# A modulation vector's last step taken from TensorE, and the vectors after it formed one place later

## The chip, the cores and the metric

The kernel runs as one program on one core of a Trainium2 chip. The metric is the device time of one execution in microseconds (us), median of three runs. Engines work side by side and meet only at semaphores: TensorE (PE in the rows; PEld is its weight load), VectorE (DVE), ScalarE (ACT), GpSimd (POOL) and SyncE (SP), whose only work here is to start transfers.

## The reference

Two blocks over 512 tokens of width 1024. The first is an attention and convolution block with a gate:

```python
x = first_block(x, p, ...)          # attention || conv, w_out, RMS norm, then x + sigmoid(x @ w_ple_gate) * e
c_act = jax.nn.silu(c)
for i in range(2):
    mod = c_act @ w_ada[i] + b_ada[i]                     # 6 vectors of 1024
    sh1, sc1, g1, sh2, sc2, g2 = jnp.split(mod, 6, axis=-1)
    h = modulate(rmsnorm(x, norm_mix_g[i]), sh1, sc1)     # h * (1 + sc1) + sh1
    m = fourier_mixer(h, w_fourier_out[0]) if i == 0 else retention_mixer(h, ...)
    x = x + g1[:, None, :] * m
    h = modulate(rmsnorm(x, norm_ffn_g[i]), sh2, sc2)
    x = x + g2[:, None, :] * swiglu(h, w_ffn_in[i], w_ffn_out[i])   # hidden width 2816
shf, scf = jnp.split(c_act @ w_ada_final + b_ada_final, 2, axis=-1)
return modulate(rmsnorm(x, final_norm_g), shf, scf)
```

There are so 14 modulation vectors of 1024 numbers, `mod[0]` to `mod[13]`: six for each layer and two for the end. Each is a 1024-vector times a 1024 x 1024 matrix of float32 (4 MB). `mod[4]` is `sc2` of layer 0, the scale of its second norm; `mod[5]` is `g2` of layer 0; `mod[11]` is `g2` of layer 1.

## The kernel before

**The weights' stream.** All weights of the matmuls lie in HBM in the order of their use, as 257 chunks of 128 x 1024 (512 KB, eight 128 x 128 weight tiles). A chunk c goes through four hands, in rings of four slots: SP loads it (`w_raw`, L346), ACT rounds it to a high part (`w_hi`, L455), POOL subtracts to get the low part in four quarters (`w_lo`, L423), and PE multiplies with both: three matmuls for each tile (lo x hi, hi x lo, hi x hi; L1785, L1788, L1789 for 512 columns, L1801 to L1805 for half tiles). SP starts the load of chunk c when POOL has finished chunk c-4; ACT splits chunk c when PE has begun chunk c-3; PE begins chunk c when all four quarters of its low part are there. Each engine runs its instructions in the written order, so SP is one queue: what stands behind a waiting load waits too.

**The modulation's stream.** The vectors' matrices come as 112 pieces of 512 KB (8 for a vector) through `ada_raw`, a ring of only two slots. A piece a is loaded by SP (L352) when VectorE has consumed piece a-2 (`ada_sum`). VectorE's step on a piece (`ada`: L992 for a vector's first, L995 for the others) multiplies the 128 x 1024 piece with one column of `cact` and adds it to `ada_acc`. After eight steps `ada_acc` holds 128 partial sums for each of the 1024 outputs, which must be summed over the partitions and turned into columns. Three ways stand in the kernel: vectors 0 to 3 (in the attention's loop) are transposed by PE (`ada_turn`); vector 4 goes through eight matmuls of 128 x 128 by one column (`ada_columns`, L1964), which stand between the tiles of the `ple` product, and VectorE adds the bias (`ada_out`, L1008); vectors 5 to 13 are turned in blocks by VectorE (`ada_fold`, L1030 transpose and L1031 sum), moved between partitions by sixteen small copies on ScalarE (`ada_move`, L796) and summed by VectorE (`ada_collect`, L1024 and L1025). The last way writes to a part of `cols`, the `ident` columns, that nobody reads after the attention.

**Where the pieces are loaded.** SP's program is written out: a load of a weight chunk, then as many pieces as stand with that chunk. `load(at, k)` does so for one chunk; `turns(n, chunks, k)` is a loop of n rounds; `until(c)` loads chunks alone. Vector 5's pieces (40 to 47) stand in the Fourier mixer, 48 to 95 with 48 chunks from `up0a`+10 on, 96 to 111 with 16 chunks from `up1a`+10 on.

**The stages.** attention (32 chunks), `out` (8), `ple` (2), `gate` (8), Fourier mixer `dft1`, `dft2`, `fout` (1, 4, 8), layer 0's swiglu `up0a` (24), `down0a` (12), `up0b` (20), `down0b` (10), retention (64), layer 1's swiglu (66). Counted from `up0a` as 0, `down0a` begins at chunk 24, `up0b` at 36, `down0b` at 56 and the retention at 66. In `down0b` (K = 10 tiles of hidden values by 8 output tiles) the first four output tiles run side by side and end at a quarter, a half, three quarters and the end of chunk 60 (from chunk 56: 32 products, then two for each tile); VectorE adds each to the residual (L1163), ScalarE squares it (L690), VectorE adds the squares (L1061). Here ScalarE's order is: the splits of chunks 60 to 64, then the first four squares, then the splits of 65 and on.

**VectorE's steps around the change.** In the mixer: two steps after `dft1`, one behind each of three Fourier groups, three before `fout`'s tiles, 8 in all (vector 5). In `up0a`: 24 steps; in `down0a`: 8 behind tiles 3 to 6; in `up0b`: 16 (4 for each of the first four rounds); in `down0b`: none. In `up1a`: 16.

Of the kernel before, what the change touches and what calls it, by code (L numbers as in the profile page):

```python
# [16 lines left out]
P = 128  # L17
# [88 lines left out]
for _name, _n in (("pre", 1), ("body", 7 * NH), ("post", 1), ("ada4", 1), ("ple", 1), ("four", 1), ("fshift", 1), ("edge", 1),  # L106
                  ("ffn0", 1), ("rnorm", 1),
                  ("ret", NH), ("ffn1", 1), ("final", 1)):
    AUX[_name] = _c
    _c += _n  # L110
# [28 lines left out]
def build(nc, W, ADA, XT, PT, COLS, DIST, ROPE, DECAY, OUT):  # L139
# [3 lines left out]
    with ctx:  # L143
# [197 lines left out]
        def _(sp):  # L341
# [103 lines left out]
        def _(act):  # L445
# [26 lines left out]
            def vector(g):  # L472

                return lambda m: mod[:, KD * g + m:KD * g + m + 1]

# [308 lines left out]
            for n in range(8):  # L784
                if n < 6:
                    split_w(flat, c0 + n + 4)
# [3 lines left out]

            def ada_move(g, at=flat):

                act.wait_ge(ada_folded, at("vector", g - 4))
                for b in range(4):
                    for q in range(4):
                        ins = act.activation(ada_quads[32 * q:32 * q + 32, :, b], ada_part[32 * b:32 * b + 32, q:32:4],  # L796
                                             ACT.Copy)
                ins.then_inc(ada_moved, 1)
# [17 lines left out]
            def swiglu(layer, v, t0):  # L816
                split_norm(4 + 2 * layer, 1 + 2 * layer, AUX[f"ffn{layer}"], t0, vector(6 * layer + 3),
                           CH[f"up{layer}a"])
                for part, n_hid in zip("ab", HALF):
# [5 lines left out]
                    if layer == 0:  # L825
                        n_pairs, g = (n_hid // 2 - first) // 2, 5 if first else 9
# [17 lines left out]
                    for n in range(n_hid):  # L844
                        if layer == 0 and part == "a" and n == 2:
                            ada_move(8)
# [125 lines left out]
        def _(dve):  # L972
# [43 lines left out]
            def ada_collect(g, at=flat):  # L1016

                dve.wait_ge(ada_moved, at("vector", g - 4))
# [367 lines left out]
            for m in range(KD):  # L1386
# [6 lines left out]
                if m == 2:  # L1393
                    ada_out(AUX["ada4"], 4)
# [67 lines left out]
            ada(k=2)  # L1462
# [10 lines left out]
            for g in range(NH):  # L1473
# [58 lines left out]
            def swiglu(layer, v, a_in, with_ada, t_in, g_in):  # L1532
                g0 = 6 * layer
                split_norm(f"ffn{layer}", v - 1, a_in, vector(g0 + 3), t_in, g_in, gain(2 + 2 * layer))
                for part, n_hid in zip("ab", HALF):
# [3 lines left out]
                    g = 5 + (0 if first else 4)  # L1539
                    if first:  # L1540
                        up_body(flat, t, j)
                    if with_ada:
                        n_pairs = (n_hid // 2 - first) // 2
                        began = steps[0]
                        with dve.Fori(0, n_pairs) as i:
                            at = At(i, tile=8, bank=2, hid=4, ada=8, adaslot=64, vector=1, eight=8, link=2)
                            ada_fold(g, at)
# [898 lines left out]
```

## Time and profile before

| | us |
|---|---|
| median of 3 runs (lowest, highest) | 1541.06 (1540.83, 1541.74) |
| the profiled execution's own time | 1540.15 |
| its span, first to last instruction | 1538.2 |
| PE busy | 1526.9 (99%) |
| POOL busy | 876.3 (57%) |
| DVE busy | 786.8 (51%) |
| ACT busy | 632.4 (41%) |

The profiled execution's span is 1.95 us shorter than its own time, and that time is 0.91 us below the median. TensorE's granted clock is 0.999 of full speed over the span. PE is busy nearly throughout, so a change counts only where PE's stream grows, shrinks or waits. PE's busy time counts the matmuls' full length, which overlap: a matmul of 512 columns is listed with 0.39 us, while the next one starts 0.23 us later. Gaps in PE's work are read best from starts.

### The profile page before, as it was taken

Reading aid. Unit: us, or ns where it says so; the run is one execution under the profiler, and the core shown is the slowest. Engines: PE = TensorE matmul, PEld = TensorE weight load, DVE = VectorE, ACT = ScalarE, POOL = GpSimd, SP = SyncE. Lnnn points to the kernel's source line nnn. Section 1 sums busy time; section 2 is a strip of 40 time slices with the busy share of each in tenths; the row PEclk is TensorE's granted clock in tenths of the full one; section 3 lists DMA queues with packets and bytes.
Section 4 is the critical chain, followed back from the end, with each engine's and each line's share of the span. In section 5 each row is a group of like instructions: output and inputs, shape, how many; then the busy total and the mean of one; then the engine's idle time right before and its main releaser. Section 6 shows DMA issues by size and latency. Waiting matters only on the chain.

```text
span 1538.2 us, 21352 instructions
## 1 busy us (share of the span) xinstructions
PE 1526.9 (99%) x7242; PEld 1276.9 (83%) x7242; DVE 786.8 (51%) x1176; ACT 632.4 (41%) x1038; POOL 876.3 (57%) x1040
## 2 busy tenths in 40 slices
PE   9999999999999999999999999999999999999997
PEld 7888888898888888888888888888889888888886
DVE  7887787876654544541554435356257454011113
ACT  7444444674533333323444334253345333122223
POOL 6555557556577766775454535526435766555551
PEclk9999999999999999999999999999999999999999
DMA  7544455335355555542232322213312553222321
GB/s 247 178 145 165 167 192 191 110 110 178 122 180 205 196 190 181 199 150 96 101 103 69 108 69 94 95 52 96 95 55 83 205 205 123 96 96 95 95 82 55
DMA packets 58267, 202.99 MB, mean 132 GB/s; under 512 B 6496, under 2 KB 8544, under 8 KB 58208
## 3 DMA queue, kind: packets, MB, share of 16 engines
q1 hardware_dynamic: 56912, 198.87, 37.8%
q10 hardware_dynamic: 1296, 3.30, 0.6%
q8 instruction: 40, 0.66, 0.2%
q14 instruction: 19, 0.16, 0.0%
HBM read 200.05 MB, written 2.10 MB: 131 GB/s over the span
## 4 chain that ended last, share of the span: by engine, by line
PE 78%; POOL 11%; issue 9%; ACT 0%; DMA 0%; DVE 0%; SPq 0%; POOLq 0%; DVEq 0%; ACTq 0%
PE banks L1785 21%; PE banks L1789 21%; PE banks L1788 21%; POOL w_lo L423 11%; PE banks L2270 2%; PE banks L2269 2%; PE banks L2266 2%; PE banks L1801 2%; PE banks L1804 2%; PE banks L1805 2%; PE banks L2306 1%; PE banks L2304 1%; PE banks L2305 1%; PE banks L2293 0%; PE banks L2292 0%
## 5 line engine op out<-in xcount | busy, mean ns | idle before, releaser
L423 POOL TENSOR_TENSOR w_lo<-w_raw,w_hi 128x256 fp32r<-128x256 f32 x1028 | 868.9, 877 | 627.8 <-ACT w_hi L455 627.7
L455 ACT ACTIVATE w_hi<-w_raw 128x1024 fp32r<-128x1024 f32 x257 | 269.9, 1057 | 582.6 <-PE banks L1785 518.8
L1785 PE MATMUL banks<-a_hi,w_lo 128*128 128x512 f32 x1224 | 479.2, 391 | 0.1
L1789 PE MATMUL banks<-a_hi,w_hi 128*128 128x512 f32 x1224 | 476.7, 389 | 0.0
L1788 PE MATMUL banks<-a_lo,w_hi 128*128 128x512 f32 x1224 | 476.6, 389 | 0.0
L1785 PEld LDWEIGHTS banks<-a_hi,w_lo 128*128 128x128 f32 x1224 | 230.1, 188 | 47.6 <-issue 0.8
L1789 PEld LDWEIGHTS banks<-a_hi,w_hi 128*128 128x128 f32 x1224 | 229.8, 188 | 47.8
L1788 PEld LDWEIGHTS banks<-a_lo,w_hi 128*128 128x128 f32 x1224 | 229.9, 188 | 47.3 <-issue 0.2
L1785 PE MATMUL banks<-b_hi,w_lo 128*128 128x512 f32 x562 | 219.6, 391 | 0.0
L1789 PE MATMUL banks<-b_hi,w_hi 128*128 128x512 f32 x562 | 218.8, 389 | 0.0
L1788 PE MATMUL banks<-b_lo,w_hi 128*128 128x512 f32 x562 | 218.8, 389 | 0.0
L995 DVE SCALAR_TENSOR_TENSOR ada_acc<-ada_raw,small,ada_acc 128x1024 f32<-128x1024 f32 x98 | 149.1, 1522 | 44.6 <-DMA ada_raw<-in_ADA 42.5
L1785 PEld LDWEIGHTS banks<-b_hi,w_lo 128*128 128x128 f32 x562 | 105.5, 188 | 22.9 <-DVE scr L1492 0.5
L1788 PEld LDWEIGHTS banks<-b_lo,w_hi 128*128 128x128 f32 x562 | 105.5, 188 | 21.9 <-issue 0.2
L1789 PEld LDWEIGHTS banks<-b_hi,w_hi 128*128 128x128 f32 x562 | 105.5, 188 | 21.9
L1163 DVE SCALAR_TENSOR_TENSOR X<-banks,mod,X 128x512 f32<-128x512 f32 x63 | 46.1, 748 | 146.8 <-PE banks L1789 146.7
L1520 DVE TENSOR_TENSOR scr<-scr,banks 128x512 f32<-128x512 f32 x44 | 30.2, 687 | 109.5 <-PE banks L1789 109.2
L1516 DVE SCALAR_TENSOR_TENSOR scr<-scr,banks 128x512 f32<-128x512 f32 x44 | 30.2, 687 | 102.2 <-ACT scr L807 102.2
L1528 DVE SCALAR_TENSOR_TENSOR b_lo<-scr,b_hi 128x512 f32 (+1 forms) x44 | 33.3, 757 | 52.1 <-ACT b_hi L814 52.1
L2269 PE MATMUL banks<-w_hi,a_lo 128*128 128x512 f32 x128 | 49.8, 389 | 0.0
L2266 PE MATMUL banks<-w_lo,a_hi 128*128 128x512 f32 x128 | 49.8, 389 | 0.0
L2270 PE MATMUL banks<-w_hi,a_hi 128*128 128x512 f32 x128 | 49.8, 389 | 0.0
(300 smaller groups left out, 1708.4 us busy)
## 6 DMA issues: line engine op xcount, KB each, us to landing
w_raw<-in_W SPq DMA_DIRECT2D x258, 512.0 KB, 3.5
ada_raw<-in_ADA SPq DMA_DIRECT2D x112, 512.0 KB, 4.2
X<-in_XT SPq DMA_DIRECT2D x8, 256.0 KB, 6.3
scr<-in_DECAY ACTq DMA_DIRECT2D x4, 448.0 KB, 3.9
out<-X SPq DMA_DIRECT2D x7, 256.0 KB, 2.2
w_raw<-in_W SPq DMA_DIRECT2D x2, 256.0 KB, 3.9
scr<-in_PT ACTq DMA_DIRECT2D x1, 512.0 KB, 4.8
scr<-in_ROPE ACTq DMA_DIRECT2D x1, 512.0 KB, 4.5
```

The lines of the kernel that those rows point to most:

```text
L423: pool.tensor_tensor(w_lo[:, c % RING, part], w_raw[:, c % RING, part], w_hi[:, c % RING, part].bitcast(fp32), ALU.subtract).then_inc(wlo, 1)
L455: act.activation(w_hi[:, c % RING, :], w_raw[:, c % RING, :], ACT.Copy).then_inc(whi, 1)
L995: ins = dve.scalar_tensor_tensor(out=ada_acc[:, :], in0=src, scalar=cact[:, f:f + 1], in1=ada_acc[:, :], op0=ALU.mult, op1=ALU.add)
L1163: ins = dve.scalar_tensor_tensor(out=X[:, m, :], in0=banks[:, BANK[t], :], scalar=mod[:, KD * g + m:KD * g + m + 1], in1=X[:, m, :], op0=A ...
L1528: dve.scalar_tensor_tensor(out=lo, in0=HD[:, n, :], scalar=0.5, in1=hi.bitcast(fp32), op0=ALU.mult, op1=ALU.subtract).then_inc(hid_ready, 1)
L1785: mm = pe.matmul(out, lo, x_hi, start=first, stop=False)
L1788: pe.matmul(out, hi, x_lo, start=False, stop=False)
L1789: mm = pe.matmul(out, hi, x_hi, start=False, stop=last)
L1801: mm = pe.matmul(out, lo, x_hi[:, part], start=first, stop=False)
L2266: mm = pe.matmul(out, a_hi[:, k, c], wl, start=(k == 0), stop=False)
L2269: pe.matmul(out, a_lo[:, k, c], wh, start=False, stop=False)
L2270: mm = pe.matmul(out, a_hi[:, k, c], wh, start=False, stop=(k == KD - 1))
```

## The change

`mod[4]` is no longer made by eight matmuls in the `ple` product: it takes the way of vectors 5 to 13, with `ada_fold(4)` on VectorE after the last Fourier group, `ada_move(4)` on ScalarE in `fout` and `ada_collect(4)` on VectorE before `fout`'s first residual. Vector 5 and all later ones move one place back: the eight steps of vector 5 go from the mixer to `up0a`, those of 8 to `down0a`, of 9 and 10 to `up0b`, and vector 11's eight steps stand, new, in `down0b`, two behind each of the output tiles 0 to 3. Vectors 12 and 13 stay in `up1a`, where vector 11 is now folded too. SP's pieces follow: none from `ple` to `fout`, 56 pieces with 56 chunks from `up0a`+10 on, so that pieces 88 to 95 (vector 11) stand with chunks 58 to 65.

```diff
--- before.py
+++ after.py
@@ SP
             straight(2, 2)
             assert pos == [CH["ple"] + 4, 5 * KD]
-            straight(*[0] * 8, 1, 1, 0, 0, 0, 1, 1, 1, 1, 1, 1)
-            assert pos[1] == 6 * KD
             until(CH["up0a"] + 10)
-            turns(6 * KD // 4, 4, 1)
+            turns(7 * KD // 4, 4, 1)
             until(CH["up1a"] + 10)
             turns(2 * KD // 4, 4, 1)
@@ ScalarE
             for n in range(8):
+                if n == 2:
+                    ada_move(4)
                 if n < 6:
                     split_w(flat, c0 + n + 4)
...
-                    if layer == 0:
-                        n_pairs, g = (n_hid // 2 - first) // 2, 5 if first else 9
+                    if layer == 0 and first:
+                        for k in range(1, n_hid // 2):
+                            up_body(flat, c + 4 * k, t + 4 * k, j + 2 * k, 5 if k == 3 else None)
+                        ada_move(6)
+                    elif layer == 0:
+                        n_pairs, g = (n_hid // 2 - first) // 2, 8
...
-                            up_body(flat, c + 4 * k, t + 4 * k, j + 2 * k, 12 + k // 4 if k in (3, 5) else None)
+                            up_body(flat, c + 4 * k, t + 4 * k, j + 2 * k, 11 + k // 2 if k in (1, 3, 5) else None)
@@ VectorE
-                if m == 2:
-                    ada_out(AUX["ada4"], 4)
             xg_lo(KD - 1)
...
             dve.wait_ge(aux_free, AUX["fshift"] + 1)
-            ada(k=2)
             t0 = TI["dft2"]
...
-                if g > 1:
-                    ada()
                 fourier_lo(g)
-                if g == 1:
-                    ada()
             t0 = TI["fout"]
-            ada(k=3)
+            ada_fold(4)
             for n in range(8):
                 if n >= 3:
                     if n == 3:
-                        dve.wait_ge(aux_free, AUX["ada4"] + 1)
+                        ada_collect(4)
+                        dve.wait_ge(ada_made, 1)
                         scale_columns(2, col("ffn", 0, KD), 4)
...
-                    if with_ada:
-                        n_pairs = (n_hid // 2 - first) // 2
+                    if with_ada and first:
+                        for k in range(1, n_hid // 2):
+                            if k in (3, 5):
+                                ada_fold(4 + k // 2)
+                            up_body(flat, t + 4 * k, j + 2 * k, 2)
+                            if k in (3, 5):
+                                ada_collect(4 + k // 2)
+                        ada(k=4)
+                        ada_fold(7)
+                    elif with_ada:
+                        n_pairs = n_hid // 4
...
                     elif layer == 0:
-                        dve.wait_ge(ada_made, 7)
+                        dve.wait_ge(ada_made, 4)
                         scale_columns(3, col("mix", KD, KD), 7)
-                        residuals(t, range(KD - 1), g0 + 5, v)
+                        for m in range(KD - 1):
+                            residuals(t, (m,), g0 + 5, v)
+                            if m < 4:
+                                ada(k=2)
                         front_end(v, t, g0 + 5)
@@ TensorE
-            def ada_columns(at, u, g):
-
-                pe.wait_ge(ada_sum, at("ada", KD * (g + 1)))
-                pe.wait_ge(aux_free, at("aux", u))
-                for f in range(KD):
-                    mm = pe.matmul(aux[:, f:f + 1], ada_acc[:, f * P:(f + 1) * P], ones[:, 0:1], start=True, stop=True)
-                mm.then_inc(aux_ready, 1)
...
-                    if m == 3:
-                        ada_columns(flat, AUX["ada4"], 4)
```

How instructions move shows at three places. The rows are the built program's; a name such as `banks<-a,b` says what is written from what, and the brackets hold the semaphores waited for.

TensorE, in the `ple` product behind the fourth output tile, before:

```order
L1785 MATMUL banks<-b_hi,w_lo 128x512
L1788 MATMUL banks<-b_lo,w_hi 128x512
L1789 MATMUL banks<-b_hi,w_hi 128x512
L1964 MATMUL banks<-ones_r,ada_acc 128x1 [waits aux_free,ada_sum]
L1964 MATMUL banks<-ones_r,ada_acc 128x1 x7
L1785 MATMUL banks<-b_hi,w_lo 128x512 [waits wlo,bank_read3]
```

and the same place after:

```order
L1956 MATMUL banks<-sqsum,ones_r 128x512 [waits aux_free,sq_added]
L1790 MATMUL banks<-b_hi,w_lo 128x512 [waits bank_read6]
L1793 MATMUL banks<-b_lo,w_hi 128x512
L1794 MATMUL banks<-b_hi,w_hi 128x512
L1790 MATMUL banks<-b_hi,w_lo 128x512
```

The eight small products are gone; nothing else moves on TensorE in the whole program.

VectorE, at the beginning of `down0b`, before (`mod` vector collected, a gain made, then residual tiles and sums of squares):

```order
L1025 TENSOR_TENSOR mod<-small,cols 128x8 [waits dve_link]
L1157 SCALAR_TENSOR_TENSOR gs<-mod,cols 128x8 [waits ada_made]
L1163 SCALAR_TENSOR_TENSOR X<-banks,mod,X 128x512 [waits tile_ready,dve_link]
L1163 SCALAR_TENSOR_TENSOR X<-banks,mod,X 128x512 [waits tile_ready] x2
L1061 TENSOR_TENSOR sqsum<-sqsum,banks 128x512 [waits bank_read4,sq_ready]
L1163 SCALAR_TENSOR_TENSOR X<-banks,mod,X 128x512 [waits tile_ready]
```

and after:

```order
L1161 SCALAR_TENSOR_TENSOR gs<-mod,cols 128x8 [waits ada_made]
L1167 SCALAR_TENSOR_TENSOR X<-banks,mod,X 128x512 [waits tile_ready,dve_link]
L996 TENSOR_SCALAR ada_acc<-ada_raw,small 128x1024 [waits ada_in0]
L999 SCALAR_TENSOR_TENSOR ada_acc<-ada_raw,small,ada_acc 128x1024 [waits ada_sum,ada_in1]
L1167 SCALAR_TENSOR_TENSOR X<-banks,mod,X 128x512 [waits tile_ready]
L999 SCALAR_TENSOR_TENSOR ada_acc<-ada_raw,small,ada_acc 128x1024 [waits ada_sum,ada_in0]
L999 SCALAR_TENSOR_TENSOR ada_acc<-ada_raw,small,ada_acc 128x1024 [waits ada_sum,ada_in1]
L1167 SCALAR_TENSOR_TENSOR X<-banks,mod,X 128x512 [waits tile_ready]
L1065 TENSOR_TENSOR sqsum<-sqsum,banks 128x512 [waits bank_read4,sq_ready]
```

Vector 11's first step (L996) now stands behind the first residual tile, whose matmuls end a quarter into chunk 60.

SyncE, one round's part of the loop that loads chunks with pieces (before: 12 rounds of four chunks from `up0a`+10; after: 14), after:

```order
L346 ISA [waits wlo]
L346 DMA w_raw<-in_W 128x1024
L350 REGISTER_ALU
L352 ISA [waits ada_sum]
L352 DMA ada_raw<-in_ADA 128x1024
L344 REGISTER_ALU
L346 ISA [waits wlo]
L346 DMA w_raw<-in_W 128x1024
```

The next chunk's load (the second L346) stands behind the wait of the piece before it. With 14 rounds this holds for chunks 58 to 65 too, where before chunks came alone.

## Rows read from the trace of the kernel before

**Rows 1.** The page, part 1: busy time of each engine.

```profile
PE 1526.9 (99%) x7242; PEld 1276.9 (83%) x7242; DVE 786.8 (51%) x1176; ACT 632.4 (41%) x1038; POOL 876.3 (57%) x1040
```

**Rows 2.** Timeline of PE in `ple`: start, us, line, operation, operands, [idle before].

```profile
262.89 1.84 PE L1964 MATMUL banks<-ones_r,ada_acc 128*128 128x1 f32 x16
264.60 0.48 PE L1785 MATMUL banks<-b_hi,w_lo 128*128 128x512 f32 x1
```

**Rows 3.** Timeline from `ple` to chunk `gate`+4, four engines.

```profile
268.47 0.15 DVE L1008 TENSOR_TENSOR mod<-banks,cols 128x8 f32<-128x8 f32 x1
...
288.11 1.04 ACT L455 ACTIVATE w_hi<-w_raw 128x1024 fp32r<-128x1024 f32 x1
...
289.23 11.64 POOL L423 TENSOR_TENSOR w_lo<-w_raw,w_hi 128x256 fp32r<-128x256 f32 x16 [9.25 <-ACT w_hi L455]
...
292.65 0.47 PE L1785 MATMUL banks<-a_hi,w_lo 128*128 128x512 f32 x1
```

**Rows 4.** Timeline, the mixer's last step, and one move and one fold's transpose later.

```profile
366.54 1.35 DVE L995 SCALAR_TENSOR_TENSOR ada_acc<-ada_raw,small,ada_acc 128x1024 f32<-128x1024 f32 x1 [5.89 <-DMA ada_raw<-in_ADA]
...
678.29 1.23 DVE L1030 STREAM_TRANSPOSE scr<-ada_acc 128x1024 f32<-128x1024 f32 x1
...
695.25 3.62 ACT L796 ACTIVATE cols<-cols 32x8 f32<-32x8 f32 x16
```

**Rows 5.** Timeline of SP's queue before `down0b`: last piece, then chunks 60 and 61.

```profile
668.18 0.33 SPq L352 DMA_DIRECT2D ada_raw<-in_ADA  x1
...
681.59 6.21 SPq L346 DMA_DIRECT2D w_raw<-in_W  x2
```

**Rows 6.** Timeline in `down0b`: first residual tile, begin of chunk 61, split of 64.

```profile
716.68 0.75 DVE L1163 SCALAR_TENSOR_TENSOR X<-banks,mod,X 128x512 f32<-128x512 f32 x1 [17.19 <-PE banks L1789]
...
720.48 0.39 PE L1785 MATMUL banks<-b_hi,w_lo 128*128 128x512 f32 x1
720.71 0.39 PE L1788 MATMUL banks<-b_lo,w_hi 128*128 128x512 f32 x1
...
720.97 1.06 ACT L455 ACTIVATE w_hi<-w_raw 128x1024 fp32r<-128x1024 f32 x1 [4.38 <-PE banks L1785]
...
722.10 2.83 POOL L423 TENSOR_TENSOR w_lo<-w_raw,w_hi 128x256 fp32r<-128x256 f32 x4 [2.61 <-ACT w_hi L455]
```

**Rows 7.** Timeline, first steps of a vector and what SP issues next.

```profile
334.57 0.75 DVE L992 TENSOR_SCALAR ada_acc<-ada_raw,small 128x1024 f32<-128x1024 f32 x1
...
335.36 0.33 SPq L352 DMA_DIRECT2D ada_raw<-in_ADA  x1
335.73 0.43 SPq L346 DMA_DIRECT2D w_raw<-in_W  x1
...
641.67 1.23 DVE L992 TENSOR_SCALAR ada_acc<-ada_raw,small 128x1024 f32<-128x1024 f32 x1
...
643.07 0.33 SPq L352 DMA_DIRECT2D ada_raw<-in_ADA  x1
```

**Rows 8.** Issue to landing, 590 to 680 us: line L352 first, line L346 second.

```profile
DMA to landing us min/median/max: 3.3/4.0/5.0
DMA to landing us min/median/max: 3.3/3.6/4.1
```

**Rows 9.** Timeline of POOL and DVE: a low part made beside two steps.

```profile
673.08 5.26 POOL L423 TENSOR_TENSOR w_lo<-w_raw,w_hi 128x256 fp32r<-128x256 f32 x4 [2.62 <-ACT w_hi L455]
674.31 3.44 DVE L995 SCALAR_TENSOR_TENSOR ada_acc<-ada_raw,small,ada_acc 128x1024 f32<-128x1024 f32 x2
```

**Rows 10.** The chain's last matmuls: start, us, engine, tile, line.

```profile
1529.59 0.71 PE banks L1845 x2
```

**Rows 11.** Stretches at the end: busy of engines, then PEclk, DMA share, GB/s.

```profile
1533.50:1534.00 0.50, 0.00 (x0) 0.00 (x0) 0.46 (x2) 0.50 (x3) 0.00 (x0) 1.00 0.00 0
1534.00:1534.50 0.50, 0.00 (x0) 0.00 (x0) 0.50 (x3) 0.50 (x2) 0.00 (x0) 0.75 0.96 326
```

**Rows 12.** Line L1978, PE's first matmuls: ns min/median/max, first and last start.

```profile
L1978 PE MATMUL banks<-ones_r x20: 274/421/579, 1.4 to 5.4; 128*128 128x128 f32 x20
```

More of the change, by code:

```diff
@@ L105 @@
 _c = 0
-for _name, _n in (("pre", 1), ("body", 7 * NH), ("post", 1), ("ada4", 1), ("ple", 1), ("four", 1), ("fshift", 1), ("edge", 1),
+for _name, _n in (("pre", 1), ("body", 7 * NH), ("post", 1), ("ple", 1), ("four", 1), ("fshift", 1), ("edge", 1),
                   ("ffn0", 1), ("rnorm", 1),
@@ L474, in vector, with ada_move @@
                 return lambda m: mod[:, KD * g + m:KD * g + m + 1]
+            def ada_move(g, at=flat):
+                act.wait_ge(ada_folded, at("vector", g - 3))
+                for b in range(4):
+                    for q in range(4):
+                        ins = act.activation(ada_quads[32 * q:32 * q + 32, :, b], ada_part[32 * b:32 * b + 32, q:32:4],
+                                             ACT.Copy)
+                ins.then_inc(ada_moved, 1)
             def split_squares(v):
@@ L788, in _ @@
                     residual_squares(4, t0, (0, 1, 2, 3) if n == 3 else (n,))
[L791 to L798, printed above, removed]
             def up_body(at, c, t, j, g=None):
@@ L1016, in ada_collect @@
             def ada_collect(g, at=flat):
-                dve.wait_ge(ada_moved, at("vector", g - 4))
+                dve.wait_ge(ada_moved, at("vector", g - 3))
                 if at.i is None:
@@ L1546, in swiglu @@
                             at = At(i, tile=8, bank=2, hid=4, ada=8, adaslot=64, vector=1, eight=8, link=2)
-                            ada_fold(g, at)
-                            for half in range(2):
-                                k = first + half
+                            ada_fold(8, at)
+                            for k in range(2):
                                 up_body(at, t + 4 * k, j + 2 * k, 2)
-                            ada_collect(g, at)
+                            ada_collect(8, at)
                         steps[0] = began + 8 * n_pairs
                         linked[0] += 2 * (n_pairs - 1)
-                        k = first + 2 * n_pairs
-                        ada_fold(g + n_pairs)
-                        up_body(flat, t + 4 * k, j + 2 * k, 2 if first else 0)
-                        ada_collect(g + n_pairs)
-                        if first:
-                            ada(k=4)
-                            ada_fold(g + 3)
+                        k = 2 * n_pairs
+                        ada_fold(8 + n_pairs)
+                        up_body(flat, t + 4 * k, j + 2 * k)
+                        ada_collect(8 + n_pairs)
                     elif first:
                         for k in range(1, n_hid // 2):
-                            if k in (3, 5):
-                                ada_fold(12 + k // 4)
+                            if k in (1, 3, 5):
+                                ada_fold(11 + k // 2)
                             up_body(flat, t + 4 * k, j + 2 * k, 2 if k < 5 else 0)
-                            if k in (3, 5):
-                                ada_collect(12 + k // 4)
+                            if k in (1, 3, 5):
+                                ada_collect(11 + k // 2)
                     else:
@@ L1576, in swiglu @@
                             if with_ada and m == 3:
-                                ada_collect(g + 3)
+                                ada_collect(7)
                             if with_ada and 3 <= m < 7:
```

3 lines of the change are left out of this document (1 added, 2 removed).

## The prediction

> **What bounds the kernel now.** I read the page's busy times first: PE is busy 1526.9 us of a span of 1538.2, 99%, and the next engine 57% [rows 1]. So time is lost or won only where PE's own stream grows, shrinks or waits, and every edit is asked one question: does a matmul start later or earlier for it? Next I read the timelines at the places that the change touches: `ple`, where PE loses eight small products [rows 2, 3]; the mixer, where VectorE loses eight steps [rows 4]; and `down0b`, where it gets eight [rows 5 to 9]. What feeds PE at each place is the chain SP load, ACT split, POOL low part. The reader is to see in it how early each link runs. In the normal course it is very early: SP issues the loads of chunks 60 and 61 at 681.59 and 687.47 (two issues in 6.21 us, the second's 0.33 us included) [rows 5], and PE begins chunk 61 only at 720.48 [rows 6]. That lead of 33 us is what the change spends.
>
> **Part 1, the eight small products.** They begin at 262.89 and the next matmul at 264.60 [rows 2]: 1.71 us of PE's stream go away. Do they stay away? PE next needs chunk `gate`+4. ACT splits it at 288.11, and POOL's low parts start at 289.23, four chunks in 11.64 us, so 2.9 for the first, done at 292.1 to 292.5; PE's first matmul with it starts at 292.65 [rows 3]. The split is not late through PE: ACT does it behind its squares of `E`, which follow VectorE's chain of residual tiles, and that chain starts from the statistics taken before the eight products. So PE would arrive 1.7 us earlier and wait for the same low part. What remains is what VectorE's chain gains, the removed `ada_out`, 0.15 us [rows 3]. I take -0.15 us; the bounds are 0 and -1.71.
>
> **Part 2, the mixer.** Eight steps and their pieces leave it. VectorE did wait there, 5.89 us for the last piece [rows 4], but PE did not wait for VectorE: with 99% busy [rows 1] there are 11 us without PE work in the whole span, most of them before its first and after its last matmul. Cost and gain: 0. Added are one fold (a transpose of 1.23 us and a sum of about the same), one move of 3.62 us on ACT [rows 4] and a collect. The move stands before the split of chunk `fout`+6, which PE needs more than ten us later; the fold takes the place of three steps. 0 us, and at most the 3.62 if the cover were gone.
>
> **Part 3, up0a to up0b and up1a.** The steps have the same numbers per stage and stand at the same places; only which vector they make differs. Vector 11's fold and move are new in `up1a`: 1.2 and 3.62 us [rows 4] beside 21.8 us of PE work per round (four chunks of 24 matmuls at 0.23 us [rows 6]). 0 us.
>
> **Part 4, down0b.** Here the cover is gone. Pieces 88 to 95 are loaded with chunks 58 to 65, by one queue, with a ring of two. Piece 90 stands behind chunk 60's load and waits for the step on piece 88. That step stands in VectorE's order behind residual tile 0, which exists a quarter into chunk 60: VectorE starts it at 716.68 [rows 6]. Behind the waiting piece stands the load of chunk 61. So a load that went out at 687.47 [rows 5] goes out after 716.68, and PE wants its low part at 720.48 [rows 6]. Nobody can hide this: PE has no other work. Step by step:
> - residual tile 0: 716.68 + 0.75 = 717.43, and step 88 starts 0.1 before its listed end, 717.3 [rows 6];
> - step 88 is a first step (L992): 0.75 us, 1.23 at worst [rows 7]. POOL has nothing to do there, so 0.75: 718.05;
> - SP sees it 0.17 us later (641.67 + 1.23 = 642.90, issue at 643.07) and issues piece 90; the chunk's load follows 0.37 later in one pair [rows 7]: 718.6, and I take 718.7;
> - landing: 3.3 to 4.1 us for a chunk, 3.3 to 5.0 for the piece that is the second of a pair; here the chunk is the second, so 4.0 [rows 8]: 722.7;
> - ACT starts 0.1 later and POOL 1.13 behind ACT (720.97 to 722.10) [rows 6]: 723.9;
> - POOL's four quarters: 2.83 alone [rows 6], 5.26 beside two steps of VectorE [rows 9]. Step 90's piece lands before POOL starts, step 91's about when it does, so one step falls beside it: 4.0, done at 727.9;
> - PE 0.1 later: 728.0.
> The stall is 728.0 - 720.48 = 7.5 us. Shortest with every smallest value (0.75, 3.3, 2.83): 5.5 us; longest (1.23, 5.0, 5.26): 10.3 us.
>
> The POOL term is where a rule weighs. The row gives 1.2 us more for each step beside it. The Trainium skill (SBUF — State Buffer, Who interferes with whom) says that GpSimd and a VectorE operation with two SBUF inputs take a shared pair of ports as an exclusive lock and the loser stands still for the whole instruction; the trace agrees, with 5.26 against 2.83 us [rows 9]. By that rule both steps would have to lie fully inside to cost 2.4, which would make the stall 8.8 instead of 7.5.
>
> Chunk 62 is loaded one step later, 1.3 to 1.5 us behind 61, and POOL does it right after 61, while PE works 5.4 us on 61: no second stall. Chunks 63 and 64 wait for steps 90 and 91, which need pieces that land by about 724: they come 5 to 7 us behind 61's load and are wanted 11 and 16 us behind it. ScalarE's first squares stand behind the split of 64, so VectorE's sum of squares waits some us and its later steps with it; tiles 4 to 6 end every 6.8 us and give it time to catch up before the half tiles. 0 us more.
>
> **Part 5, the clock.** The last matmuls end at 1529.59 + 0.71 = 1530.30 [rows 10]. The granted clock is still 1.00 in the stretch to 1534.0, and 0.75 on average from there to 1534.5, so it fell from 2.4 to 1.2 GHz about 3.95 us after PE's last work [rows 11]. PE would stand still for 7 us: it should fall here too. What it costs to come back is seen at the start: 20 matmuls of one shape between 1.4 and 5.4 us, median 421 ns, fastest 274 [rows 12], so most of some 4 us ran at the low level. Half of 3.7 us is lost: 1.8 us, bounds 0 (it does not fall) and 3.7 (twice as long).
>
> The Trainium skill (TensorE: Matmul & The Clock Gate, Part 1: The HAM clock gate) says that the half rate is the default and that only activity releases it, which speaks against every new stall on PE. By it 1.8 us belong to the stall; without it the sum would be 7.4 us.
>
> **The sum.** -0.15 + 0 + 0 + 7.5 + 1.8 = +9.15 us. The profiled execution took 1540.15 us, its span 1538.2; it would become 1549.3 with a span near 1547.4. The median of the runs shown is 0.91 above that execution: 1541.06 + 9.15 = 1550.2 us.
>
> **The rivals.**
> A. Stall without the clock's fall. For it: PE has done dense work for 700 us, and the fall at the end came 3.95 us after its last matmul with 7 us to spare here, which is not much. Against it: those same 3.95. Time: 1541.06 - 0.15 + 7.5 = 1548.4.
> B. The delay spreads. VectorE's steps 90 to 95 wait each for a piece that is loaded behind the last one; if its sums of squares come late for the half tiles, PE waits again at the statistics, and a low clock may be entered twice. For it: ScalarE's squares behind the split of 64 and a ring of two. Against: 20 us of slack until tile 7. Price: another 4 us: 1554.
> C. Not slower: chunk 61 isn't held. The price of the stall is a difference of two times, and it decides from one point: if step 88 ended before 711 (720.48 less 9.3, the way from issue to PE), nothing would wait. For that the step would have to run ahead of tile 0, which VectorE's order excludes, or SP's wait would have to count otherwise than I read it. Then either the 1.71 us are kept: 1539.3; or they go into the wait for `gate`+4: 1540.9, no change.
>
> **How the numbers follow.** My forecast (stall and clock) has 0.60, A 0.22, B 0.09, C 0.09 (0.05 with the gain, 0.04 without). The predicted time is the likeliest's, 1550.2. Its own range, from the stall's 5.5 to 10.3 us and the clock's 0 to 3.7, is 1546.4 to 1554.9; what lies near both ends at once is unlikely, so 1546 to 1554 holds 8 in 10 with A inside and C and most of B left out. About 0.2%, 3 us, is what a measurement tells from no change: slower by more 0.91, within 0.05, faster 0.04.
>
> **What would show it.** In the profile after: L1964 gone and a wait or a late start at chunk `gate`+4, with the mixer's begin moved by less than 0.5 us; at SP one weight load some 38 us behind the one before it, right after a piece's load; ACT's split of chunk 61 waiting for a DMA; one PE wait of about 7 us on POOL's low part near 720; a granted clock below 1.00 in the few us behind it; PE's total busy time as before or a little above, by the slower matmuls. Wrong: no PE gap near 720 (C), a clock of 1.00 throughout (A), or a second gap between 730 and 750 (B). If `gate`+4 is begun 1.5 us earlier, part 1 was wrong.

## The result, and the profile after

| | before | after |
|---|---|---|
| median, us (lowest to highest) | 1540.88 (1540.72 to 1541.74), 6 runs | 1551.19 (1550.55 to 1553.64), 6 runs |
| ratio of after to before | | 1.0068, 95% interval 1.0055 to 1.0081 |

The change makes the kernel 10.3 us slower; 1550.2 was forecast, with a range of 1546 to 1554. The profile shown here is of the execution of 1553.64 us (span 1551.5), the longest of the six. A second profile of the same kernel, of an execution of 1550.56 us, stands under the experiments.

The page's busy times answer to [rows 1]:

```profile
PE 1530.7 (99%) x7226; PEld 1278.8 (82%) x7226; DVE 792.5 (51%) x1179; ACT 635.5 (41%) x1054; POOL 873.7 (56%) x1040
```

PE's share has not changed, and its time has grown by 3.8 us although eight products are gone. The busy line doesn't say what happened; 13.3 us were added to the span. The list of PE's waits does (what waited and for whom: total us, times, longest us):

```profile
PE banks L1790 <- POOL w_lo L421: 8.7, 2, 8.1
PE banks L1975 <- DVE ones_r L1187: 1.4, 1, 1.4
PE banks L1961 <- DVE b_lo L1401: 1.0, 1, 1.0
```

The 1.4 stands before too (there at L1978). New are the wait of 8.1 us for a low part and, at the gate, the 1.0 for L1961 and the rest of the 8.7. The timeline of `down0b` has it (start us, duration us, what; in brackets the idle time before it and what ended it), to be held against [rows 5 to 7]. First SP, whose queue it begins in:

```profile
683.71 0.33 SPq L346 DMA_DIRECT2D w_raw<-in_W  x1
720.38 0.33 SPq L352 DMA_DIRECT2D ada_raw<-in_ADA  x1
720.97 0.33 SPq L346 DMA_DIRECT2D w_raw<-in_W  x1
721.78 0.33 SPq L352 DMA_DIRECT2D ada_raw<-in_ADA  x1
722.67 0.33 SPq L346 DMA_DIRECT2D w_raw<-in_W  x1
```

Chunk 60's load went out at 683.71 and chunk 61's at 720.97, 37 us later and right behind piece 90. Before, these two were 5.9 us apart [rows 5]. Then the other engines:

```profile
718.80 0.75 DVE L1167 SCALAR_TENSOR_TENSOR X<-banks,mod,X 128x512 f32<-128x512 f32 x1 [17.32 <-PE banks L1794]
719.47 0.75 DVE L996 TENSOR_SCALAR ada_acc<-ada_raw,small 128x1024 f32<-128x1024 f32 x1
722.37 0.39 PE L1794 MATMUL banks<-b_hi,w_hi 128*128 128x512 f32 x1
725.79 1.06 ACT L453 ACTIVATE w_hi<-w_raw 128x1024 fp32r<-128x1024 f32 x1 [22.43 <-DMA w_raw<-in_W]
726.92 5.13 POOL L421 TENSOR_TENSOR w_lo<-w_raw,w_hi 128x256 fp32r<-128x256 f32 x6 [20.66 <-ACT w_hi L453]
730.83 0.76 PE L1790 MATMUL banks<-b_hi,w_lo 128*128 128x512 f32 x1 [8.07 <-POOL w_lo L421]
731.39 0.63 PE L1793 MATMUL banks<-b_lo,w_hi 128*128 128x512 f32 x1
...
736.93 0.44 PE L1794 MATMUL banks<-b_hi,w_hi 128*128 128x512 f32 x1
```

The rows stand in order of time, and the chain reads so: residual tile 0, step 88, SP's two issues, the landing, ACT, POOL, PE. ACT had been idle for 22.43 us and the bracket names the DMA. PE's last matmul of chunk 60 starts at 722.37 and the next one at 730.83. Until 736.93 the matmuls start 0.43 us apart (731.39, 731.82, 732.24, ...) instead of 0.227. The windows show the clock that goes with it (window, its length, busy time of PE, PEld, DVE, ACT, POOL, granted clock, DMA share, GB/s), first around the stall, then at chunk `gate`+4:

```profile
716.00:732.00 16.00, 7.93 (x33) 6.27 (x32) 6.66 (x7) 2.12 (x3) 5.08 (x6) 0.84 0.65 230
732.00:740.00 8.00, 8.00 (x27) 6.32 (x26) 2.94 (x2) 3.64 (x5) 6.99 (x11) 0.69 0.17 67
740.00:760.00 20.00, 19.98 (x109) 17.28 (x108) 10.63 (x15) 5.75 (x8) 9.43 (x12) 1.00 0.75 263
...
293.00:296.00 3.00, 2.92 (x7) 2.31 (x8) 2.02 (x4) 2.95 (x4) 3.00 (x5) 0.55 0.53 176
296.00:299.00 3.00, 3.00 (x13) 2.49 (x12) 3.00 (x6) 2.99 (x6) 3.00 (x5) 0.88 0.49 176
```

Looked at more closely, the clock fell within the stall, not behind it:

```profile
726.00:727.00 1.00, 0.00 (x0) 0.00 (x0) 0.00 (x0) 0.84 (x1) 0.08 (x1) 0.89 1.03 418
727.00:728.00 1.00, 0.00 (x0) 0.00 (x0) 0.63 (x1) 0.00 (x0) 1.00 (x2) 0.50 1.07 356
```

A mean of 0.89 puts the fall at about 726.8, some 4.0 us after the end of PE's last matmul (722.37 + 0.39).

There were two falls to the lower level (1.2 of 2.4 GHz) in this execution: the expected one, and one at chunk `gate`+4, which nobody had expected. PE waits twice there, 1.0 us for the sum of squares (L1961) and then 0.66 us for the low part:

```profile
292.03 0.39 PE L1794 MATMUL banks<-a_hi,w_hi 128*128 128x512 f32 x1
293.07 0.59 PE L1790 MATMUL banks<-a_hi,w_lo 128*128 128x512 f32 x1 [0.66 <-POOL w_lo L421]
```

Behind 293.07 the starts are 0.42 us apart until 296.44.

The span's 13.3 us are so: 0.46 by which PE was already later at 209 us, long before the change (start to start, 209.42 against 208.96); some 1.6 for the fall at `gate`+4; the stall, 730.83 - (720.48 + 2.12) = 8.2, where 2.12 is what chunk 61 was late by then for the first two reasons; and the fall behind it, 14 or 15 matmuls at 0.43 instead of 0.227, about 2.9. These are 13.2.

### The profile page after: what moved, and what is told of

Its sections match the earlier page's. It is cut to its first block, busy times and chain, and to the rows that moved or that the text cites. A ratio compares the mean times of both kernels' runs of the same rounds, so it can differ in the third digit from the quotient of the medians.

```text
span 1551.5 us, 21343 instructions
## 1 busy us (share of the span) xinstructions
PE 1530.7 (99%) x7226; PEld 1278.8 (82%) x7226; DVE 792.5 (51%) x1179; ACT 635.5 (41%) x1054; POOL 873.7 (56%) x1040
## 4 chain that ended last, share of the span: by engine, by line
PE 52%; POOL 27%; issue 19%; ACT 0%; DMA 0%; POOLq 0%; DVE 0%; SPq 0%; DVEq 0%; ACTq 0%
POOL w_lo L421 27%; PE banks L1790 13%; PE banks L1793 13%; PE banks L1794 13%; PE banks L2265 2%; PE banks L2264 2%; PE banks L2261 2%; PE banks L1806 1%; PE banks L1809 1%; PE banks L1810 1%; PE banks L2301 1%; PE banks L2300 1%; PE banks L2299 1%; PE banks L2288 0%; PE banks L2287 0%
## 5 line engine op out<-in xcount | busy, mean ns | idle before, releaser
L1526 DVE SCALAR_TENSOR_TENSOR b_lo<-scr,b_hi 128x512 fp32r<-128x512 f32 (+1 forms) x44 | 34.3, 780 | 51.8 <-ACT b_hi L814 51.8
```

The costliest lines, as they stand in the source:

```text
L1526: dve.scalar_tensor_tensor(out=lo, in0=HD[:, n, :], scalar=0.5, in1=hi.bitcast(fp32), op0=ALU.mult, op1=ALU.subtract).then_inc(hid_ready, 1)
```

## The experiments

All are edits of the kernel after unless said otherwise, and each has runs of the kernel before beside it (medians 1541.27 for e1 to e4, 1541.22 for e5 to e8, 1541.09 for e9 and e10). The theory is the prediction's: SP's one queue puts chunk 61's load behind piece 90, piece 90 behind step 88, and step 88 behind residual tile 0; PE stands still and the clock falls. The rivals: VectorE's eight steps in `down0b` themselves are what costs; and the removed 1.71 us of products should have come back as a gain.

**Four of vector 11's steps taken ahead, into `up0b`'s last round (e1_four_ahead).**

```diff
-                        up_body(flat, t + 4 * k, j + 2 * k)
+                        up_body(flat, t + 4 * k, j + 2 * k, 2)
...
-                            if m < 4:
+                            if m < 2:
                                 ada(k=2)
```

> The changed kernel, with four of vector 11's eight steps (pieces 88 to 91) taken from down0b's tiles 2 and 3 to the last round of up0b, so that the first step behind tile 0 is that of piece 92; SP's program is the changed one. Queue theory (the step on piece 88, late behind tile 0, holds piece 90 and with it the load of chunk 61): now piece 94, which stands with chunk 64, is the first to wait for a step in down0b, and chunk 65's load stands behind it, four chunks ahead of its use: no stall, no low clock near 720. Time that of the kernel before, 1540.9, or up to 1.7 more where the clock falls at chunk gate+4: 1541 to 1542.6. Rival, VectorE theory (the steps themselves, their ports or the late sums of squares in down0b cost the time): half of the steps still stand there, so about half of 10 us stays: 1546.

Measured: 1540.79 (1540.14 to 1541.46), ratio to before 0.9997 [0.9988, 1.0006]. The whole loss is gone, and nothing of the eight products' 1.71 us shows as a gain: the time can't be told from no change. PE's row from 700 to 760 is full:

```profile
700.00:760.00 60.00, 59.98 (x330) 52.11 (x329) 27.50 (x44) 21.77 (x34) 31.12 (x39) 1.00 0.37 131
```

**One step ahead (e2_one_ahead).** With step 88 done early, piece 90 goes out at 698.62 already; piece 91 waits for step 89, which now stands behind tile 0, and behind piece 91 stands the load of chunk 62, which PE wants 5.4 us later.

```diff
                         up_body(flat, t + 4 * k, j + 2 * k)
+                        ada()
...
-                                ada(k=2)
+                                ada(k=2 if m else 1)
```

> The changed kernel with one step, that of piece 88, taken from down0b to the end of up0b's last round. Queue theory: piece 90 is free, piece 91 (with chunk 61) waits for the step on piece 89 behind tile 0, and chunk 62's load stands behind it. In the changed kernel's trace 10.6 us lie between the end of the holding step and PE's first matmul with the held chunk. The step on 89 would end 2.0 us behind the start of tile 0's residual, PE wants chunk 62 9.2 us behind that start: a stall of 2.0 + 10.6 - 9.2 = 3.4 us. With the clock's fall, if so short a wait lets it fall, up to 2 more. Time 1541.5 + 3.4 = 1545, up to 1547. Rival (any piece held costs the whole stall, or VectorE's steps are the cost): 1550 to 1551.

Measured: 1545.37 (1544.01 to 1547.68), ratio 1.0027 [1.0018, 1.0036]. The profile has the stall, shortened and moved by one chunk, and a low clock behind it as well:

```profile
PE banks L1791 <- POOL w_lo L421: 4.1, 2, 3.5
```

```profile
730.00:735.00 5.00, 4.30 (x12) 3.47 (x13) 1.15 (x2) 2.92 (x5) 5.00 (x8) 0.66 0.04 17
735.00:740.00 5.00, 5.00 (x24) 4.14 (x23) 4.21 (x5) 0.60 (x1) 3.15 (x2) 1.00 0.60 212
```

3.5 us of waiting were enough: the granted clock is 1.00 until 730.5 and 0.76 on average from there to 731.0, so it fell at about the moment at which PE began again (730.70). The starts are 0.43 apart from 731.26 to 733.83; with the one at 730.70 these are eight slow matmuls, 1.6 us.

**The pieces alone moved in SP's program (e7_pieces_later).** All eight steps stay where the change put them.

```diff
-            turns(7 * KD // 4, 4, 1)
+            turns(6 * KD // 4, 4, 1)
+            straight(1, 1, 0, 0, 0, 0, 0, 0, 2, 2, 2)
+            assert pos[1] == 12 * KD
```

> The changed kernel with only SyncE's program altered: pieces 90 to 95 do not stand with chunks 60 to 65 but two each behind chunks 66, 67 and 68, so that chunks 61 to 66 are issued as early as in the kernel before. All of vector 11's eight steps stay in down0b on VectorE. Queue theory: no weight load is held for long (67 and on have a lead of six chunks), so no stall and no low clock: 1541 to 1542, as the kernel before, although VectorE waits in down0b for its pieces and its residual tiles run late until tile 5. VectorE theory (steps, ports or late sums in down0b cost the time): near the changed kernel, 1548 to 1551, or a new wait of TensorE at the statistics behind down0b.

Measured: 1541.22 (1540.91 to 1541.85), ratio 1.0000 [0.9991, 1.0009]. SP and VectorE, from its timeline:

```profile
682.20 32.96 SPq L346 DMA_DIRECT2D w_raw<-in_W  x7
719.45 2.00 SPq L352 DMA_DIRECT2D ada_raw<-in_ADA  x2
721.72 0.33 SPq L346 DMA_DIRECT2D w_raw<-in_W  x1
...
722.82 1.28 DVE L1001 SCALAR_TENSOR_TENSOR ada_acc<-ada_raw,small,ada_acc 128x1024 f32<-128x1024 f32 x1 [1.06 <-DMA ada_raw<-in_ADA]
726.56 1.32 DVE L1001 SCALAR_TENSOR_TENSOR ada_acc<-ada_raw,small,ada_acc 128x1024 f32<-128x1024 f32 x1 [2.45 <-DMA ada_raw<-in_ADA]
```

Seven weight loads run through before the piece that waits. VectorE now waits for its pieces, and PE for nothing: 59.98 of 60 us. So the steps in `down0b` cost nothing, and the place of their pieces in SP's queue costs everything. This is the shortest proof of the mechanism: one line of SP's order and the same work.

**PE kept at work during the stall (e3_filler).** 34 matmuls of 512 columns into a bank that nobody reads then, before chunk 61.

```diff
+            def filler(n):
+                if n == 39:
+                    for _ in range(34):
+                        pe.matmul(banks[:, 6, :], ones_r[:, :], a_hi[:, 0, :], start=True, stop=True)
...
-                         split=None if first else v)
+                         split=None if first else v, hook=filler if layer == 0 and not first else None)
```

> The changed kernel with 34 matmuls of 512 columns, whose results nobody reads, put on TensorE between its last matmul of chunk 60 and its first of chunk 61 (7.7 us at 0.227). Theory: the wait for chunk 61's low part stays as it is, since nothing of the chain that feeds it is touched, but TensorE works through nearly all of it, so the granted clock stays at 2.4 GHz behind it and the slow matmuls (24 of the 27 below full clock) are gone: 1.5 to 3 us less than the changed kernel, 1548.5 to 1549.7. Rival (the low clock is not the consequence of the idle time, or costs nothing): as the changed kernel, 1551.2. Rival (the filler is work on the bound engine): longer than the changed kernel by up to 7.7.

Measured: 1549.90 (1548.25 to 1550.81), ratio 1.0056 [1.0042, 1.0069].

```profile
721.62 8.10 PE L2220 MATMUL banks<-a_hi,ones_r 128*128 128x512 f32 x34
729.55 0.39 PE L1790 MATMUL banks<-b_hi,w_lo 128*128 128x512 f32 x1
```

Chunk 61 begins at 729.55, as late as in the kernel after (729.46 in its second profile, below), since its load is late too (720.00); but the clock stays at 1.00 from 700 to 760 and the matmuls behind start 0.23 apart at once. The median is 0.2 above what was expected and 1.3 below the one of the kernel after, which was measured in another series; the intervals of the two ratios overlap, so the times alone don't show the saving, and the profile's clock does show that the fall is gone. Most of the loss is the wait, and a smaller part the clock.

**One product instead of eight, in the kernel before (e4_one_product).** It leaves out seven eighths of the sums of `mod[4]`.

```diff
-                for f in range(KD):
+                for f in range(1):
```

> The kernel before with only the first of the eight small products of vector 4 (seven eighths of that vector's sums are left out). Nothing else is changed. My theory: TensorE gets 1.5 us ahead in ple and waits that much longer for the low part of chunk gate+4 and for the sum of squares just before it, which VectorE and ScalarE make at the same time as ever: the matmul that begins gate+4 starts within 0.2 us of where it starts before; time 1540.9, and 1.5 more (1542.4) if the clock falls behind that wait as it did in the changed kernel's profile. Rival (TensorE is 99% busy, so what is taken from it is won): 1539.4.

Measured: 1541.97 (1541.36 to 1542.95), ratio 1.0004 [0.9995, 1.0013]. No gain, and the median is even 0.7 higher. PE's new waits in its timeline:

```profile
291.46 0.51 PE L1956 MATMUL banks<-b_lo,ones_r 128*128 128x512 f32 x1 [0.71 <-DVE b_lo L1399]
293.52 0.47 PE L1785 MATMUL banks<-a_hi,w_lo 128*128 128x512 f32 x1 [0.63 <-POOL w_lo L423]
```

Chunk `gate`+4 begins 0.87 us later than before (293.52 against 292.65), where 0.2 had been expected. PE was already 0.91 us later near 209 us, ahead of the edit (209.87 against 208.96; the table below), so seven of the eight products moved this start by nothing. The clock stays at 1.00 in this profile.

**The 1.71 us collected (e5_early_split).** If a late split of chunk `gate`+4 is what eats them, an earlier one must give them back. To e1 are added:

```diff
+                if m == 6:
+                    split_w(flat, CH["gate"] + 4)
...
-                if n not in (3, 7):
+                if n not in (0, 3, 7):
                     split_w(flat, c0 + n + 4)
...
-                if n == 30:
+                if n == 34:
                     pe.wait_ge(sum_lo, 1)
```

ACT splits the chunk before the squares of `E`, and PE does the two statistics' matmuls four products later, when the sum of squares is there.

> The changed kernel with four of vector 11's steps in up0b's last round (as in the run four_ahead), and two more edits at the gate: ScalarE splits chunk gate+4 before it rounds the eighth residual tile instead of behind the squares of E, and TensorE takes the statistics of E four products later (after 34 instead of 30). Theory: the eight small products are a gain of 1.7 us that the late split of gate+4 swallows; with the split early TensorE no longer waits there, so that 1.7 of the products and some 0.3 of the wait that the kernel before had are won: 1539.2 against 1541.2, and the matmul that begins gate+4 starts about 2 us earlier. Rival (another link of the same chain, the sum of squares or the gate tiles on VectorE, is as late): no gain, 1540.8, with a wait in its place before dft1.

Measured: 1539.64 (1539.34 to 1540.36), ratio 0.9990 [0.9981, 0.9999]: 1.6 us below before by the medians (2.0 had been expected), with its highest time under the lowest of before's 33 (1540.60), and 1.15 below e1's median of the other series. It is the best of all kernels here. PE is full at the gate:

```profile
290.00:293.00 3.00, 3.00 (x15) 2.46 (x14) 1.68 (x3) 2.02 (x5) 0.22 (x1) 1.00 0.00 0
293.00:296.00 3.00, 3.00 (x15) 2.47 (x14) 0.47 (x2) 2.96 (x4) 2.61 (x4) 1.00 0.00 0
```

**The same two edits in the kernel before (e6_before_early_split).** The diff is e5's gate part.

> The kernel before, with the eight products kept, and only the two edits at the gate: chunk gate+4 split early, the statistics of E four products later. Theory: TensorE waited 0.3 us for gate+4 there, so 0.3 us is all there is to win without the products' removal: 1540.9 against 1541.2, which these runs hardly tell from no change. Rival (the edits themselves are the gain of the run with both): 1539.2.

Measured: 1540.93 (1540.00 to 1541.44), ratio 0.9998 [0.9989, 1.0007]. Before, the eight products filled PE until the low part was ready, so an early split alone brings next to nothing. Only both together do: 1.3 us between e6 and e5.

**The early split with the statistics at the old place (e8_split_old_hook).** e5 with `n == 30` again.

> As the run with the early split and the steps ahead, but with the statistics of E at their old place (after 30 products). In the changed kernel TensorE waited 1.0 us there for VectorE's low part of the sum of squares and 0.7 for gate+4. Theory: the wait for gate+4 goes and the one for the sum, 1.0 to 1.8 us, stays, so the kernel is 0.2 to 0.9 us faster than the kernel before: 1540.3 to 1541, with the wait at L1961 the only one near 290. Rival (the statistics' place does not matter): as the run with both edits, 1539.2.

Measured: 1542.19 (1540.88 to 1544.11), ratio 1.0007 [0.9998, 1.0016]. This was a miss, and the spread of 3.2 us is the odd thing. The profile is of the execution of 1540.88:

```profile
PE banks L1963 <- DVE b_lo L1403: 2.4, 1, 2.4
```

The two short waits have become one that is longer than both. The reason is on ScalarE: the split that was put first delays its rounding of the eighth residual tile and its squares, and with them VectorE's low part of the sum (first in the kernel after, then in e8):

```profile
290.27 0.69 DVE L1401 TENSOR_TENSOR b_lo<-sqsum,b_hi 128x512 fp32r<-128x512 f32 x1 [0.70 <-ACT b_hi L688]
...
291.03 0.69 DVE L1403 TENSOR_TENSOR b_lo<-sqsum,b_hi 128x512 fp32r<-128x512 f32 x1 [0.69 <-ACT b_hi L690]
```

e8's profile is 0.69 us ahead of that of the kernel after near 209 us (208.73 against 209.42), so the sum comes 1.45 us later, by as much as the wait has grown (0.95 to 2.41); PE reaches the statistics no sooner. The expectation had taken the sum as unmoved. In e5 the sum is as late, and the statistics' new place hides it. The clock is 1.00 there in this execution; the mean granted clock is 0.998 in it and 0.997 in the four from 1543.13 up, which suggests that it falls in these; no profile of one of them shows it.

**PE kept at work in that wait (e10_gate_filler).** e8 and twelve matmuls before the wait.

```diff
                 if n == 30:
+                    pe.wait_ge(aux_free, flat("aux", AUX["ple"]))
+                    for _ in range(12):
+                        pe.matmul(aux, ones_r[:, :], a_hi[:, 0, :], start=True, stop=True)
                     pe.wait_ge(sum_lo, 1)
```

> The kernel with the early split and the old place of the statistics' matmuls (e8), plus 12 matmuls of 512 columns on PE while it waits there for the sum of squares (2.7 us; they write the two statistics' bank before the statistics' own matmuls overwrite it, so nothing of the result changes). e8 had a wait of 2.4 us there and times from 1540.88 to 1544.11 us, its profile (1540.88) without a fall of the clock. Theory 1 (in e8's slower executions the clock falls behind that wait, some 1.6 to 3 us): with PE kept at work all executions come to 1540.5 to 1541.5, median about 1541.0, and the spread shrinks to about 1 us. Rival (the spread has another cause, such as the order of DMAs): the spread of some 3 us and a median near 1542.2 stay.

Measured: 1541.68 (1541.15 to 1542.27), ratio 1.0004 [0.9995, 1.0013].

```profile
290.20 2.96 PE L2099 MATMUL banks<-a_hi,ones_r 128*128 128x512 f32 x12
293.00 0.40 PE L1963 MATMUL banks<-b_lo,ones_r 128*128 128x512 f32 x1
```

The spread shrank from 3.2 to 1.1 us, as the theory of the clock says, and its highest time is 1.8 us below e8's, though in another series. The median is 0.7 above what was expected: the late sum of e8 is still there, and the filler adds its rest to it. In its profile PE is also 1.0 us later than in e8's some 30 us from the start (the first matmul of L1991 at 29.78 against 28.82), before any edit.

**One measure for all profiles.** Such a shift lies in every pair of them: before any edit takes effect they differ by up to 1.1 us, and that alone moves a kernel's time by what some of these edits are worth. What the gate costs is therefore read between two starts of the same profile, of the matmul behind the last turned block near 209 us and of `dft1`'s first (L2140 before, L2135 after):

| | near 209 | `dft1` | between | against before |
|---|---|---|---|---|
| before | 208.96 | 314.51 | 105.55 | |
| after, second profile | 209.41 | 314.91 | 105.50 | -0.05 |
| after, first profile (clock fell) | 209.42 | 316.52 | 107.10 | +1.55 |
| e1 | 209.17 | 314.68 | 105.51 | -0.04 |
| e4 | 209.87 | 315.38 | 105.51 | -0.04 |
| e5 | 209.49 | 312.88 | 103.39 | -2.16 |
| e6 | 209.60 | 314.79 | 105.19 | -0.36 |
| e8 | 208.73 | 314.80 | 106.07 | +0.52 |
| e10 | 209.72 | 315.93 | 106.21 | +0.66 |

Taking the products away is worth 0.05 us, the early split alone 0.36, both with the later statistics 2.16, and the split with the statistics at the old place costs half a microsecond. Part of e5's 2.16 is lost again behind the gate, in waits of 0.2 us (L2137, for a sum of squares) and 0.3 us (L1792, for a low part) among others; between the medians of e1 and e5 1.15 us are left.

**The changed kernel once more (e9_after_again).** No edit.

> The changed kernel once more. In its first profile the clock fell twice: behind the stall at chunk 61 and, not foreseen, at chunk gate+4, where 7 matmuls or so ran at the low level for some 1.6 us; that execution took 1553.64 us, the others 1550.55 to 1551.66. Theory 1 (the fall at gate+4 is occasional, and only the one at chunk 61 belongs to every execution): the median stays at 1551 +- 0.5; if this profile is of an execution below 1552, the granted clock is 1.00 from 290 to 300 us and below 1 only behind the stall. Rival (the fall at gate+4 is always there, and the 1553.64 has another cause): the clock falls near 293 us again, in an execution of about 1551.

Measured: 1552.09 (1550.56 to 1554.00, five runs), ratio 1.0073 [1.0059, 1.0087]. The median is 0.6 above the band that was expected. The profile is of the execution of 1550.56 us, span 1548.6:

```profile
PE banks L1790 <- POOL w_lo L421: 8.8, 2, 8.2
```

```profile
293.00:296.00 3.00, 2.94 (x13) 2.48 (x14) 2.02 (x4) 2.95 (x4) 3.00 (x5) 1.00 0.55 175
...
724.00:732.00 8.00, 2.54 (x6) 2.08 (x7) 2.29 (x2) 3.17 (x3) 6.44 (x8) 0.59 0.96 359
732.00:740.00 8.00, 8.00 (x36) 6.56 (x36) 4.78 (x3) 2.59 (x4) 5.67 (x9) 0.98 0.03 9
```

The same two gaps at the gate (starts 1.35 and 1.03 us apart) and no fall there: the first profile's fall does not belong to every execution. And behind the same stall the low level lasts for 2.7 us of PE's work here (729.46 to 732.16, seven matmuls 0.43 apart, 1.4 us lost) against 6.1 us in the first profile. The two profiles differ by 2.9 us in span, 1.6 of it at the gate and 1.5 here; the stalls differ by 0.1 the other way. The fall itself came as late in the stall as in the first profile: the granted clock is 1.00 until 725.5 and 0.50 from there, 4.2 us after the end of PE's last matmul (720.92 + 0.39). The changed kernel's eleven times go with the mean granted clock: 1550.56 and 1550.64 at 0.997, 1552.1 and 1552.3 at 0.995, 1553.6 and 1554.0 at 0.994.

## Why the prediction was right, point by point

- **Part 1, the eight products: right, and shown.** Chunk `gate`+4 was not begun earlier: 293.07 against 292.65, which is 0.42 later, the start's offset of 0.46. The gain up to `dft1` is 0.05 us, taken 0.15. e4 removes seven of the products alone and gains nothing; e1 has them removed and stands at 0.9997. e5 shows the reason: with the split early and the statistics later PE is 2.16 us ahead at `dft1`, the 1.71 and 0.45 more. Not foreseen was that PE would wait first for the sum of squares (1.0 us) and only then for the low part (0.7), nor that the idle time left behind isn't harmless: two waits of about a microsecond in place of full work let the clock fall in one of two profiles of the kernel after, for 1.6 us.
- **Parts 2 and 3, the mixer and the stages to `up1a`: right.** No PE wait stands there, and e1, which keeps all of it, is equal to before.
- **Part 4, `down0b`: the mechanism right, the size 7.5 against 8.2 us.** Each link was where it was put. Tile 0 to SP's load: 718.80 + 0.75 to 720.97 is 1.4, against 717.43 to 718.7, 1.3 forecast. The landing term was the mis-sized one: ACT starts 4.8 after the issue, where 4.0 and 0.1 had been taken. POOL took 3.8 for four quarters, taken 4.0: one VectorE step fell beside it, as forecast (727.37, 1.35 us), and the quarter beside it took 1.71 us where those alone took 0.72. (Two small slips: the shortest stall adds up to 5.6 and not 5.5, and for rival C step 88 would have had to end before 710.5, since 0.65 us lie between its end and the issue.) e7 shows the queue as the cause, and e2 gives the dose: one step ahead takes 4.7 us off the wait.
- **No second stall: right.** Chunks 62 to 65 arrive in time, and the PE row of 740 to 760 is full (19.98 of 20). Rival B's second stall did not come, though its picture of a low clock entered twice did come, at another place.
- **Part 5, the clock: right in kind; 1.8 us against 1.4 and 2.9.** Rival A (no fall) is excluded by both profiles, and by e2 even for a wait of 3.5 us. The fall came 4.0 and 4.2 us after PE's last work; 3.95 had been read at the end of the kernel before. The size isn't one number: it differs from one execution to the next. That 1.8 lies between is partly luck, since its working is weak: it takes the matmuls from 1.4 to 5.4 us for a time at the low level, and the windows give a granted clock of 1.00 there. Only the durations speak for it (weight loads with a median of 333 ns, as the 0.33 us in the slow stretch behind the stall, against 0.19 at full clock), and 3.7 us stands in no row. e3, which keeps the clock up, lies 1.3 below by the medians.
- **Rival C, not slower: excluded.** Step 88 began at 719.47, behind tile 0.

The sum of 9.15 against 10.3 measured in the first comparison: 0.7 of the difference is the stall, and the rest is put down to the clock, which varies between executions; two profiles of eleven executions can't split it further. That the median came within 1.0 us of the forecast is luck in that share.

## What to carry to other kernels

When steps are moved, list what each of them issues and frees, and go through the queue in which its transfers stand: one waiting load holds every load written behind it, and the price is what the last of these is late, not what the step lasts. Work taken off the busiest engine counts only if what it needs next is already there; look for its next wait first, move that producer too (e5), and see what the move delays in turn (e8), or the time is only turned into idle time. And short idle stretches on TensorE may cost more than themselves.

## What had not been expected of the hardware

- The clock fell after two gaps of about 1 us within 3 us (starts 1.34 and 1.04 apart) in one profile and not in another of the same program with the same gaps, and not behind one wait of 2.4 us in e8's profile. In the long waits it fell with PE idle for 4.0 and 4.2 us (the two profiles of the kernel after) and in e2 after about 3.6, as PE began again.
- After the same stall PE worked at the low level for 2.7 us in one execution and 6.1 us in another. Times that spread by more than 3 us went with such waits (e2: 3.7, e8: 3.2, after: 3.1 and 3.4; e1: 1.3, e5: 1.0). It is no sure sign: the kernel before spreads by 2.05 in 27 runs, e3, whose stall is filled, by 2.6, and the waits at the gate remain in e1 and e7 (0.9).
- A chunk whose load was the second of a pair took 4.8 us until ACT began on it, though SP had issued nothing between 683.71 and its pair at 720.38 and 720.97; 4.9 in the second profile (719.52 to 724.43), and 5.9 for chunk 62 in e2 (720.79 to 726.74). Each time SP issued two more loads within 2 us of it, and from 722 to 724 the DMA share is 1.01 in the first profile. That the loads slowed each other is likely, but no run separates them.
